# A hybrid encoder layer on one core: the input x is turned on VectorE instead of TensorE, the token scale is applied to the projection's outputs, and the pooling columns of the weights are rounded on GpSimd

## The reference

```python
h = rmsnorm(x, norm1_g)                   # x * rsqrt(mean(x*x) + eps) * g, per token
proj = h @ w_in                           # 1024 -> 512 q, 128 k, 128 v, 512 pooling columns
q = apply_axial_rope(rmsnorm(q, q_norm_g), cos, sin)
k = apply_axial_rope(rmsnorm(k, k_norm_g), cos, sin)
a = block_swept_gqa(q, k, v)              # 8 query heads, 2 key heads, bidirectional
p = multiscale_pool(u, w_pool, pool_scale)
x = x + jnp.concatenate([a, p], axis=-1) @ w_out
h2 = rmsnorm(x, norm2_g)
x = x + jnp.square(jax.nn.relu(h2 @ w_up)) @ w_down
```

## Time and profile before

| | us |
|---|---|
| median of 3 runs | 1500.82 |
| span of the profiled execution, first to last instruction | 1499.2 |
| PE busy | 1490.5 (99%) |
| DVE busy | 1015.6 (68%) |
| ACT busy | 718.0 (48%) |
| POOL busy | 394.7 (26%) |

### The profile page before, as it was taken

One profiled execution on the slowest core, in us unless ns is written; L12 is line 12 of the kernel. 1 busy time (PEld: TensorE's weight loads), 2 busy tenths in 40 slices (PEclk: granted clock), 3 DMA queues, 4 the chain that ended last, 5 costly groups with the idle time before them and its releaser, 6 DMA issues.

```text
span 1499.2 us, 23419 instructions
## 1 busy us (share of the span) xinstructions
PE 1490.5 (99%) x8031; PEld 1328.7 (89%) x8031; DVE 1015.6 (68%) x1287; ACT 718.0 (48%) x1215; POOL 394.7 (26%) x348
## 2 busy tenths in 40 slices
PE   9999999999999999999999999999999999999999
PEld 8999988888878889999999999999888888888887
DVE  7434489999965567445445444548888878878875
ACT  6323289999943335555445455546332323223220
POOL 3356379988940000000000000000411311311300
PEclk9999999999999999999999999999999999999999
DMA  6110021100145737523333432438743443442434
GB/s 237 50 36 18 18 78 29 29 11 11 33 171 182 266 142 305 236 101 143 135 128 112 156 138 101 146 132 314 266 151 119 133 154 104 143 158 94 144 99 182
DMA packets 69113, 195.19 MB, mean 130 GB/s; under 512 B 5560, under 2 KB 7744, under 8 KB 68928
## 3 DMA queue, kind: packets, MB, share of 16 engines
q1 hardware_dynamic: 66992, 183.36, 34.8%
q10 hardware_dynamic: 2064, 11.08, 1.8%
HBM read 119.97 MB, written 67.63 MB: 125 GB/s over the span
## 4 chain that ended last, share of the span: by engine, by line
PE 93%; ACT 2%; POOL 2%; DVE 1%; issue 1%; DMA 0%; SPq 0%; ACTq 0%; POOLq 0%; DVEq 0%
PE ps L794 24%; PE ps L796 23%; PE ps L795 23%; PE ps L1096 6%; PE ps L974 4%; PE ps L1106 3%; PE ps L956 2%; PE ps L958 2%; PE ps L989 2%; PE ps L990 2%; ACT prob L1327 1%; PE ps L1116 1%; PE ps L803 1%; POOL prob L2401 0%; ACT pThi L1232 0%
## 5 line engine op out<-in xcount | busy, mean ns | idle before, releaser
L794 PE MATMUL ps<-h,wuhi 128*128 128x384 f32 (+1 forms) x904 | 301.3, 333 | 0.2 <-issue 0.2
L796 PE MATMUL ps<-h,wulo 128*128 128x384 f32 (+1 forms) x904 | 301.1, 333 | 0.0
L795 PE MATMUL ps<-h,wuhi 128*128 128x384 f32 (+1 forms) x904 | 301.1, 333 | 0.0
L794 PE MATMUL ps<-wdhi,hidhi 128*128 128x512 f32 x672 | 261.5, 389 | 0.1
L796 PE MATMUL ps<-wdhi,hidlo 128*128 128x512 f32 x672 | 261.4, 389 | 0.0
L795 PE MATMUL ps<-wdlo,hidhi 128*128 128x512 f32 x672 | 261.4, 389 | 0.0
L2202 DVE TENSOR_TENSOR yacc<-yacc,ps 128x1024 f32<-128x1024 f32 x167 | 203.3, 1217 | 77.1 <-PE ps L796 77.0
L1232 ACT ACTIVATE hidhi<-hin 128x1024 fp32r<-128x1024 f32 (+1 forms) x72 | 86.9, 1207 | 300.8 <-PE ps L796 291.7
L2116 DVE TENSOR_TENSOR u<-u,ps 128x384 f32<-128x384 f32 x96 | 53.1, 553 | 181.2 <-PE ps L796 181.1
L794 PEld LDWEIGHTS ps<-h,wuhi 128*128 128x128 f32 x904 | 169.7, 188 | 0.6 <-issue 0.4
L795 PEld LDWEIGHTS ps<-h,wuhi 128*128 128x128 f32 x904 | 169.7, 188 | 0.0
(11 more groups left out here) (221 smaller groups left out, 2822.1 us busy)
## 6 DMA issues: line engine op xcount, KB each, us to landing
hd<-hout SPq DMA_DIRECT2D x64, 384.0 KB, 3.2
hin<-hd SPq DMA_DIRECT2D x48, 512.0 KB, 3.7
hd<-hout SPq DMA_DIRECT2D x32, 576.0 KB, 2.8
hin<-hd SPq DMA_DIRECT2D x24, 768.0 KB, 4.3
wuraw<-in_w_up SPq DMA_DIRECT2D x17, 1024.0 KB, 6.0
wdraw<-in_w_down SPq DMA_DIRECT2D x8, 2048.0 KB, 9.5
h<-h2d ACTq DMA_DIRECT2D x7, 1536.0 KB, 10.9
x2in<-in_x SPq DMA_DIRECT2D x12, 512.0 KB, 3.4
```

Source lines behind the costliest of these rows:

```text
L794: pe.matmul(out, w_hi, m_hi, start=start, stop=False, skip_group_check=resumed)
L795: pe.matmul(out, w_hi, m_lo, start=False, stop=False, skip_group_check=resumed)
L796: return pe.matmul(out, w_lo, m_hi, start=False, stop=stop, skip_group_check=resumed)
```

## The change

- x is no longer scaled ahead of the product. `scale_x`, `transpose_x`, the buffer `xs` and the transposes' PSUM banks go. DVE turns the raw tile in 32x32 blocks (`turn_x`) from `xin` to `xT`, both in SBUF. For this x is loaded differently: four transfers per tile, each to 32 partitions, with four pieces of 1 KB per partition. The turned tile has feature 8p+k in partition p, so the weights are loaded with rows permuted the same way.
- `split_hT` on ACT and DVE reads `xT` in SBUF instead of PSUM.
- The rows of x are loaded a second time (`load_rows`), straight into the junk area of `up`, for the sum of squares. `square_x(t)` now comes one tile later in ACT's list. A new load waits for the square before it.
- The token factors `rs` (one column per tile) are applied by ACT in `copy_qkv`, which now waits for them, and by DVE in `split_v`. For the pooling columns, where tokens lie along the row, the factors of two tiles go out to DRAM and come back copied to all partitions (`turn_rs` on SP), and DVE applies them in `save_u_columns`, which moves from ACT to DVE.
- `split_wi_u`, the rounding of the pooling columns, moves from ACT to POOL, ahead of the work on q and k, four blocks before `norm_x(1)` and four behind it.
- `project_qkv` alternates between banks 0, 1 and 2, 3. 11 warming matmuls in a row instead of 7 and 7. The gain is loaded as a column and needs no transpose. `ident` is loaded later.

The core of the diff:

```diff
-            def transpose_x(t):
-                pe.wait_ge(xs_done, t + 1)
-
-                pe.wait_ge(hT_lo, t)
-                for k in range(KT):
-                    mm = pe.transpose(psw[:, k * P:(k + 1) * P], xs[:, k * P:(k + 1) * P], ident[:])
-                mm.then_inc(xT_done, 1)
...
+        def quarter_of(t, q):
+
+            return x[t * P:(t + 1) * P, q * 256:q * 256 + 256].rearrange("(b t) c -> t b c", b=4)
+
+        def blocks_in(i, k0=0, k1=KT):
+            return xin[:, i].rearrange("p (b c k) -> p k b c", b=4, k=KT)[:, k0:k1]
+
+        def blocks_out(k0=0, k1=KT):
+            return xT[:, k0:k1].rearrange("p k (b t) -> p k b t", b=4)
...
+            def load_x(t):
+
+                if t >= 2:
+                    sp.wait_ge(xT_done, t - 1)
+                for q in range(4):
+                    sp.dma_start(quarter_in(t % 2, q), quarter_of(t, q)).then_inc(x_in[t % 2], 16)
+
+            def load_rows(t):
+
+                if t:
+                    sp.wait_ge(ssx_done, t)
+                sp.dma_start(stat_area(), x[t * P:(t + 1) * P].rearrange("t (g c) -> t g c", g=GROUPS)).then_inc(xn_in, 16)
...
+            def turn_rs(p):
+
+                sp.wait_ge(rsx_done, 2 * p + 2)
+                sp.dma_start(rsd[p], rs[:, 2 * p:2 * p + 2]).then_inc(rs_out, 16)
+                if p >= 2:
+                    sp.wait_ge(u_saved, FIRST + p - 1)
+                sp.wait_ge(rs_out, 16 * (p + 1))
+                if p:
+                    sp.wait_ge(rs_in, 16 * p)
+                sp.dma_start(rsb[:, p % 2], rsd[p].rearrange("t i -> (t i)").partition_broadcast(P)
+                             ).then_inc(rs_in, 16)
...
+            for k in range(3):
                 load_wi(k)
...
+            load_x(1)
+            for k in range(3, KT):
                 load_wi(k)
...
+            load_rows(0)
+            load_wi_u(0)
+            load_wi_u(1)
+            load_x(2)
             sp.dma_start(gqkb[:], gqk.partition_broadcast(P)).then_inc(gqk_in, 16)
...
+            load_rope(0)
+            load_rows(1)
+            load_x(3)
+            sp.dma_start(ident[:], ident_d).then_inc(ident_in, 16)
+            load_rope(1)
+            turn_rs(0)
+            load_rows(2)
...
             def first_pair():
-                copy_qkv(0, 2)
+                square_x(1)
+                copy_qkv(0, 0)
                 square_qk(0)
-                for k in range(KT):
-                    split_wi_u(k)
-                square_x(3, 1)
-                copy_qkv(1, 4)
+                copy_qkv(1, 2)
                 square_qk(1)
                 split_hT(2, 2)
+                square_x(2)
                 split_hT(3, 3)
-                square_x(4, 0)
+                square_x(3)
                 save_qkT(0)
-                save_u_columns(0, 1)
                 save_qkT(1)
...
+            def turn_x(t):
+                dve.wait_ge(x_in[t % 2], 64 * (t // 2) + 64)
+
+                dve.wait_ge(hT_hi, t)
+                dve.wait_ge(hT_lo, t)
+                dve.transpose(blocks_out(), blocks_in(t % 2)).then_inc(xT_done, 1)
...
             def first_pair():
-                split_v(0, 3)
-                sum_squares(0)
-                scale_x(2, 0)
                 for k in range(KT // 2):
                     split_wi_u(k)
-                scale_qk(0)
+                split_v(0, 1)
+                sum_squares(0)
                 for k in range(KT // 2, KT):
                     split_wi_u(k)
-                split_v(1, 5)
+                scale_qk(0)
                 dve.wait_ge(gq_scaled, 1)
                 gain_qk(0)
+                split_v(1, 3)
                 sum_squares(1)
                 split_hT(2, 2)
-                scale_x(3, 1)
+                turn_x(3)
                 rotate(0, 0)
                 scale_qk(1)
                 gain_qk(1)
                 split_hT(3, 3)
+                turn_x(4)
                 rotate(1, 1)
-                scale_x(4, 0)
+                save_u_columns(0)
...
+            norm_x(0)
+            pool.wait_ge(g1_in, 16)
+            for k in range(KT // 2):
+                split_wi_u(k)
             norm_x(1)
-            norm_x(2)
+            for k in range(KT // 2, KT):
+                split_wi_u(k)
...
-                    opens = isinstance(n, int) and t < 2
-                    if not (last and i >= 1) and not opens:
-                        norm_x(t + 3)
                     pool.wait_ge(qk_summed, FIRST + t + 1)
                     pool.wait_ge(qn_done, FIRST + t)
                     rsqrt_mean(rsqk[:], msqk[:], ssqk[:], epsqk[:], msqk_done, rsqk_done, FIRST + t)
-                    if opens:
-                        norm_x(t + 3)
+                    if t + 2 < TT:
+                        norm_x(t + 2)
                     pool.wait_ge(qg_done, t + 1)
```

313 lines of the change are left out of this document (138 added, 175 removed).

## The result

The changed kernel takes 1515.8 us (median, 1515.2 to 1520.0), the kernel before beside it 1500.8 us: a ratio of 1.0103, 95% interval 1.0089 to 1.0118. I had forecast 1500.3 us with a range up to 1505.0, so the prediction was wrong, on the side to which I had given a chance of 0.20. The span of the profiled execution is 1514.0 us, 14.8 us more than before.

What follows compares the result with a forecast made beforehand. PE's list was taken to bound the kernel behind 41.66 us, the side chain feeding its q/k transposes ahead of that. 9.0 us gained less 8.5 lost gave 0.5 us less, 1500.3 us by the median; range 1494.0 to 1505.0 us.

Steps and rivals of the forecast that it cites:

- a loop through the scale of tile 0, ACT's list and POOL's list: Start: copy_qkv(1) waits for tile 0's scale (34.95 us), delaying square_x(2), norm_x(2) and tile 0's sine (ending 41.8 us).
- They land at 25.5 us: Start: second-load rows of tile 1 land at 25.5 us behind a full queue moving 0.385 MB per us; bounds 21.2 and 26.9.
- Four roundings at 0.74 us: Start, POOL: four split_wi_u behind norm_x(1), 0.74 us each, ending at 30.6 us.
- the contention with 0 to 1.6 us: Start: POOL's roundings and DVE's work slow each other, 0 to 1.6 us; taken as none, kept in the range.
- `square_x(2)` at 37.4 us: Start, ACT: squares of tile 2 begin at 37.4 us, behind square and split_hT(2), and take 1.3 us.
- Tile 1's transposes at 50.2 us: First pair: PE's transposes of q and k of tile 1 come at 50.2 us instead of 41.66.
- The first QKV product is led by DVE's list as before: Start, PE: the first QKV product was given no close sum, since DVE's list sets its pace as before.
- The cold clock: Rival, first pair: PE's idling drops its clock, costing 1.7 us; with slow small pieces (1.4) 1503.4 us; chance 0.14.
- Behind 41.66 us, 9.0 us gained: Steady projection: eight tiles at 1.14 us (9.1), plus 0.3 idle, less 0.4 for late transposes, give 9.0 us.
- my rival: Slow `turn_x`, later pairs: PE waits from a turn of 2.1 us; at 3.2 us the kernel takes 1511.5 us; chance 0.12.
- Nothing behind the projection: Start of attention: the last save_u_columns delays POOL by about 2.5 us, where next scores don't need it yet; priced at nothing.
- 8.5 us lost in the forecast: Ahead of 41.66 us: the delayed side chain moves PE's transpose of tile 1 to 50.2 us, 8.5 us lost.

Runs made afterwards that it cites:

- g1_widepieces: Kernel before, with x from tile 1 on in four transfers of 1 KB pieces, each to all 128 partitions: 1501.5 us, ratio 1.0003.
- c4_plainload: Changed kernel with x loaded as before, one transfer per tile with 4 KB per partition instead of four quarters: 1512.5 us, ratio 1.0072.
- c3_order: Changed kernel with the engines' lists for the first tiles reordered, copy of tile 0 ahead of squares of tile 1, ident loaded early: 1512.9 us, ratio 1.0077.
- d2_norows: Changed kernel without the second load of the token rows, squares taken from the tile loaded for the turn: 1512.7 us, ratio 1.0075.
- e1_steady: Changed kernel, start untouched, with DVE's work from tile 2 on in another order, odd tile's sums earlier and turn later: 1513.5 us, ratio 1.0086.
- e4_poolround: Kernel before with only the roundings of the pooling columns moved from ACT to POOL: 1505.8 us, ratio 1.0039.
- d1_pieces: Kernel before, with x from tile 1 on in four transfers to 32 partitions each, in 1 KB pieces: 1505.7 us, ratio 1.0033.
- f3_filler: Changed kernel with unread matmuls (14 and 9) in PE's two waits for the rotations of tiles 0 and 1: 1518.3 us, ratio 1.0109.

## Why the prediction was wrong, step by step

- **Where the kernel is bound, and which waits the change brings: right, but for SP's.** PE idle ahead of both transposes of the first pair, ended by DVE's addition; the copy of tile 0 behind the second squares; copies 8.34 us apart; a loop through the scale of tile 0, ACT's list and POOL's list. What failed were sizes, nearly all in the same direction, and one wait that was missing, that of SP's queue (below).
- **"They land at 25.5 us": 29.3 us.** This is the first step that failed, and the largest, 3.8 us. It passed my upper bound of 26.9. I priced the queue at 0.385 MB per us from weight loads to 128 partitions and let the small pieces be a quarter slower. I looked at the size of the pieces, and what counts is that a quarter goes to 32 partitions (g1_widepieces): while quarters are on their way the queue moves little more than half the rate. With plain loads in their place the rows are there at 25.61 us (c4_plainload). That they were issued at 19.3 us and not at 17.8, since SP waited for the square of tile 0, adds nothing that the record shows. Nor did the queue keep its order to the end, which my chain took for granted: two of tile 3's quarters, issued behind the rows, landed ahead of them, at 28.5 and 29.1 us.
- **Four roundings at 0.74 us: 0.95 us each**, beside DVE's splits. I had named the contention with 0 to 1.6 us and took none. Rows of before with a POOL instruction beside a DVE one stood in my own text. 0.8 us on the path, and 0.3 us more from `gqkb` and the sums; with the landing head factors of tile 0 at 36.3 us instead of 31.4.
- **`square_x(2)` at 37.4 us: 43.3 us.** I let it wait only for ACT's list. Its rows are issued behind `turn_rs(0)`, that is behind a wait of SP for the norm of tile 1 and a transfer to DRAM. I had named each wait of ACT and POOL and not SP's queue. Since POOL was late by then too, 0.9 us of it arrive: sine of tile 0 at 45.3 us instead of 39.5 plus the 4.9 us above.
- **Tile 1's transposes at 50.2 us: 57.0 us.** 5.9 us from tile 0, 0.9 us from `turn_x(4)`, 2.1 us instead of 1.2.
- **"The first QKV product is led by DVE's list as before": 2.0 us later.** PE goes on to the next product at 21.20 us instead of 19.18. It costs nothing here, since the copy of tile 0 comes at 30.36 us. In c3_order and d2_norows, where the squares are out of its way, that copy waits for PE until 24.56 and 23.63 us, against 19.37 before.
- **The cold clock.** Priced at 1.7 us and put into a rival; it costs 1.6 us. It was no alternative to the forecast but a consequence of it, since the forecast itself had PE idle twice. It belonged into the sum.
- **Behind 41.66 us, 9.0 us gained: 5.1 us.** Two sizes. The price of a tile's transposes was 1.14 us by the distance in the last pair; with the waits gone (e1_steady) pairs are 2.0, 2.0, 2.0 and 1.5 us shorter than before, so it is 1.0 us or less, 7.5 us for all. And `turn_x` takes 2.14 us, just where my rival had PE begin to wait (2.1): 2.4 us, by e1_steady. That rival had the mechanism and the threshold right.
- **Nothing behind the projection: 2.8 us.** Not foreseen, and not explained. One PE wait of 1.7 us follows from ACT's wait for a store, which is 1.6 us longer than before while the DMA queues are full in both kernels. It comes with every kernel that has the changed projection, and the place of the tensors in DRAM isn't the reason. What is, stays open.
- **The part with the roundings.** I priced it only as a term of the chain. Alone it costs 4.8 us (e4_poolround), as much as a third of the whole loss.
- **No luck in it.** The errors don't cancel: but for the clock, which came out at 1.6 us for 1.7, every term went against the forecast.

In sum: 8.5 us lost in the forecast, and 3.8 + 0.8 + 0.3 + 0.9 + 0.9 = 6.7 us more up to tile 1's transposes, 1.6 us of clock, 3.9 us less gained, 2.8 us behind: 15.0 us more than the forecast's -0.5. That gives 14.5 us, and the spans differ by 14.8. The terms up to tile 2 are read from one profile, and by the spread told above another execution could give them other sizes.

## What to carry to other kernels

Before a load or an operation is moved, go through the list of each engine and of the issuing queue and ask which instruction that waits for a load now stands ahead of the critical chain. Here there were four (ACT's squares, POOL's roundings, DVE's turn, SP's own wait), and where one was removed the trace showed the next. A change that frees the bound engine in the steady part can be kept there and left out of the first tiles, where the loads set the pace: in that form this one is worth 0.3%. Price a load by the partitions that it reaches, not by its bytes alone. Where a forecast contains idle time of TensorE, its clock belongs into the same sum.

## What the hardware showed that I had not expected

- A 32x32 block turn of 128 x 1024 floats on DVE takes 2.14 us with the source at every eighth element and 1.25 us with 32 in a row, whereas the subtraction of the same size takes 1.22 us in both kernels.
- Transfers to 32 partitions hold a full queue at 213 to 235 GB/s (220 to 291 in d1_pieces), whereas the same 128 KB in the same pieces of 1 KB to 128 partitions leave it at 352 to 414, about as much as rows of 3 to 4 KB (380 to 420). A weight load whose DRAM rows jump in two levels over the partitions moved 100 GB/s with the engines busy two tenths of the time.
- `tensor_scalar` of 128 x 512 on POOL takes 0.68 us alone and 0.95 to 1.00 us beside DVE's splits of the same tensors, which go from 0.68 to 1.0 us and more.
- With the quarters at the start the time itself varies more: 4.8 us between executions of the changed kernel, 1.6 us before. The landing of the same load moved by 6.6 us between kernels with the same order of loads (29.30 in the changed kernel, 35.90 in f3_filler), and by 7.6 us between e1_steady (28.31) and f3_filler. What moves it isn't known.
- A transfer that is issued later can land earlier: the rows of tile 1, issued at 19.29 us to 128 partitions, landed at 29.3 us, two transfers to 32 partitions issued behind them at 28.5 and 29.1 us.
